# Two token norms and a layer norm whose sums over features are added up on VectorE before TensorE sums over partitions

## The reference

```python
def rms_norm(x, g):
    y = xf * lax.rsqrt(jnp.mean(xf * xf, axis=-1, keepdims=True) + EPS)
    return y * g

def first_block(x, mem, ...):
    mem_n = rms_norm(mem, mem_norm_g)
    h = rms_norm(x, norm_g[i])
    proj = h @ dn_w_in                 # then gated delta rule, cross attention to mem_n, output projection
    ...
    x = x + y @ w_out

def second_block(x, w_in, ...):
    proj = h @ w_in                    # then pooling mixer and sparse attention
    ...
    mix = concatenate([out_pool, out_attn]) @ w_out
    h = layer_norm(ALPHA * h + mix, ln1_g, ln1_b)
    ffn = peer_ffn(h, ...)             # product keys, experts; the longest stage of the kernel
    return layer_norm(ALPHA * h + ffn, ln2_g, ln2_b)

def layer_norm(x, g, b):
    mu = mean(x); var = mean(square(x - mu))
    return (x - mu) * lax.rsqrt(var + LN_EPS) * g + b
```

## Time and profile before

| | us |
|---|---|
| median of 3 runs | 3026.83 |
| lowest and highest | 3018.61 to 3031.2 |
| the profiled execution | 3026.03 |
| its span | 3024.1 |
| TensorE busy, matmul | 2846.4 (94%) |
| VectorE busy | 1903.4 (63%) |
| ScalarE busy | 1408.8 (47%) |
| GpSimd busy | 362.9 (12%) |

### The profile page before, as it was taken

How to read it: one execution, slowest core, us unless ns; L and a number is a source line. 1 busy time by engine, 2 the same in 40 slices (tenths; PEclk the granted TensorE clock), 3 DMA queues, 4 the chain that set the end, 5 groups by cost and what they waited for, 6 DMA issues and landing times.

```text
span 3024.1 us, 46453 instructions
## 1 busy us (share of the span) xinstructions
PE 2846.4 (94%) x19394; PEld 2681.0 (89%) x19394; DVE 1903.4 (63%) x2801; ACT 1408.8 (47%) x2399; POOL 362.9 (12%) x338
## 2 busy tenths in 40 slices
PE   6999998798999999999989999998999999999996
PEld 6999998687888999999988999998887899988775
DVE  5546647642333544656456855776888888878886
ACT  5346544355555433443335204433555555545554
POOL 0000010011112000002200002222122111112210
PEclk9999999899999999999999999999999999999998
DMA  4444435422232554444434458998999988889984
GB/s 185 169 157 145 171 103 178 150 98 73 78 100 94 204 181 169 167 168 158 157 127 156 152 203 312 371 362 325 366 361 363 357 326 317 324 333 345 357 338 142
DMA packets 112048, 668.47 MB, mean 221 GB/s; under 512 B 28336, under 2 KB 28552, under 8 KB 33920
## 3 DMA queue, kind: packets, MB, share of 16 engines
q1 hardware_dynamic: 86976, 496.93, 45.4%
q0 software_dynamic: 23712, 164.11, 14.8%
q10 hardware_dynamic: 1152, 4.47, 0.4%
HBM read 651.54 MB, written 13.30 MB: 220 GB/s over the span
## 4 chain that ended last, share of the span: by engine, by line
PE 66%; DVE 13%; DMA 10%; ACT 7%; issue 2%; SPq 0%; POOL 0%; DVEq 0%; ACTq 0%
PE PS L1001 66%; DMA raw<-in_pv 8%; DVE WL L1626 5%; DVE m L1617 3%; ACT WH L2304 3%; ACT m L2289 2%; DMA m<-in_pv,keep 1%; DVE m L2129 1%; ACT L2289 1%; DVE m L1817 1%; DMA raw<-in_w_kv 1%; DVE m L1814 0%; ACT m L2290 0%; PE PS L1004 0%; DVE m_896r L2222 0%
## 5 line engine op out<-in xcount | busy, mean ns | idle before, releaser
L1626 DVE TENSOR_TENSOR WL<-raw,WH 128x1024 fp32r<-128x1024 f32 x804 | 985.5, 1233 | 672.8 <-ACT WH L2304 671.9
L2304 ACT CAST WH<-raw 128x1024 fp32r<-128x1024 f32 x804 | 837.3, 1046 | 571.2 <-PE PS L1001 371.6
L1001 PE MATMUL PS<-m_4096r,WH 128*128 128x256 f32 x5184 | 997.9, 293 | 31.1 <-DVE m_4096r L1617 11.5
L1001 PEld LDWEIGHTS PS<-m_4096r,WH 128*128 128x128 f32 x5184 | 827.1, 196 | 54.7 <-issue 13.2
L1001 PE MATMUL PS<-m_4096r,WL 128*128 128x256 f32 x2592 | 743.5, 287 | 0.0
L1001 PE MATMUL PS<-m_8192r,WH 128*128 128x256 f32 (+1 forms) x2560 | 561.1, 313 | 16.7 <-issue 11.1
L1001 PE MATMUL PS<-WH,m_896r 128*128 128x512 f32 x1536 | 524.1, 394 | 24.6 <-DVE m_896r L2222 24.5
L1001 PEld LDWEIGHTS PS<-m_4096r,WL 128*128 128x128 f32 x2592 | 507.1, 196 | 0.0
L1001 PEld LDWEIGHTS PS<-m_8192r,WH 128*128 128x128 f32 x2560 | 398.6, 194 | 19.6 <-issue 11.7
L1001 PE MATMUL PS<-m_8192r,WL 128*128 128x192 f32 (+1 forms) x1792 | 405.1, 273 | 0.0
L1001 PE MATMUL PS<-WL,m_896r 128*128 128x512 f32 x1024 | 401.5, 392 | 0.0
(11 more groups left out here) (228 smaller groups left out, 1869.7 us busy)
## 6 DMA issues: line engine op xcount, KB each, us to landing
raw<-in_pu SPq DMA_DIRECT2D x128, 1024.0 KB, 6.9
raw<-in_pv SPq DMA_DIRECT2D x128, 1024.0 KB, 8.7
raw<-in_w_qkv SPq DMA_DIRECT2D x48, 1024.0 KB, 4.8
raw<-in_w_o SPq DMA_DIRECT2D x48, 1024.0 KB, 4.8
raw<-in_w SPq DMA_DIRECT2D x40, 1024.0 KB, 4.8
raw<-in_w_z SPq DMA_DIRECT2D x32, 1024.0 KB, 4.9
raw<-in_w_kv SPq DMA_DIRECT2D x16, 1024.0 KB, 4.8
raw<-in_w_q SPq DMA_DIRECT2D x16, 1024.0 KB, 4.8
```

Source lines behind the costliest of these rows:

```text
L1001: return e.matmul(o, l, x, start=start, stop=stop)
L1626: tt(WL[:, k, :], raw[:, n % NRAW, h * 1024:h * 1024 + 1024], WH[:, k, :].bitcast(F), ALU.subtract).then_inc(S["lo"], 1)
L2304: e.copy(WH[:, k, :], raw[:, n % NRAW, h * 1024:h * 1024 + 1024]).then_inc(S["hi"], 1)
```

## The change

Four tiles are added to one on VectorE with a `tensor_reduce` over a strided view (`over_tiles`: element t of tiles k, k+1, k+2, k+3, which lie 1 KB apart), and TensorE makes one matmul with ones on the result.

- First norms: `n_square` on VectorE, behind each square of ScalarE, writes a quarter's sum into `N_PART`, and `n_sum` makes 4 matmuls instead of 16. TensorE waits on `n_part`.
- Mean of six tiles: one addition over all six behind `r1` of the sixth, one matmul instead of 6.
- Statistics: for tiles 0 to 3, 4 to 7 and 8 to 11 VectorE makes two additions (deviations, squares) at the place of `stat(3)`, `stat(7)` and `stat(11)`, with two matmuls each on TensorE there; tiles 12 to 15 are summed one by one as before. 14 matmuls instead of 32. ScalarE's square into a buffer of squares waits until the additions of the four before are done.

The two lists of steps that get a new name are left out below.

```diff
--- before.py
+++ after.py
@@ -193,10 +193,9 @@
                 yield
         if first:
             self.do("begin")
-        for kt in range(16):
-            self.do("n_sum", first, kt)
-            if kt % 4 == 3:
-                yield
+        for c in range(4):
+            self.do("n_sum", first, c)
+            yield
         self.do("n_root", first)
         yield
         for c in range(4):
@@ -391,11 +390,10 @@
             yield
 
     def statistics(self, st):
-        for m in range(6):
-            while st["r"] <= m:
-                yield
+        while st["r"] <= 5:
             yield
-            self.do("mean", m)
+        yield
+        self.do("mean")
         yield
         for m in range(17):
             while m < 16 and st["r"] <= m:
@@ -611,7 +609,7 @@
     "x_high": (("n_hi", 32), ("y_hi", 9), ("x1_hi", 16), ("att_hi", 8), ("pm_hi", 8), ("h2_hi", 8)),
     "x_low": (("n_lo", 32), ("y_lo", 9), ("x1_lo", 16), ("att_lo", 8), ("pm_lo", 8), ("h2_lo", 8)),
     "small_pe": (("sg_turn", 1), ("sg_sum", 1), ("rn_sum", 1), ("bias_mm", 1), ("wi_turn", 1), ("pm", 8), ("mean", 1),
-                 ("stat", 16)),
+                 ("stat", 1)),
     "small_dve": (("sg_min", 1), ("sg_g", 1), ("sg_gc", 2), ("keep", 1), ("bias_v", 1), ("ki", 1), ("ki_copy", 1), ("wi", 1),
                   ("mask", 2), ("ln1_var", 1), ("ln1_rs", 1)),
     "small_act": (("sg_act", 7), ("rn_root", 1), ("ln1_mu", 1), ("ln1_sd", 1)),
@@ -741,6 +739,7 @@
         N_GAIN = {True: "mem_g", False: "norm_g"}
         N_BANK = {True: 2, False: 3}
         N_LOAD = {True: "mem", False: "x"}
+        N_PART = {True: f(132, 1024), False: f(136, 1024)}
         MK, MV, XQ, XA, SQ = f(112, 2048), f(120, 2048), f(64, 2048), f(132, 2048), f(80, 2048)
         MV3 = MV.rearrange("p (m c) -> p m c", m=2)
         HN_X = {"k": MK, "q": XQ}
@@ -861,6 +860,8 @@
         PING = [f(26, 256), f(28, 256)]
         PW = f(88, 2048).rearrange("p (g d) -> p g d", g=8)
         CM, MU, RS, MR = f(80, 256), f(81, 256), f(82, 256), f(83, 256)
+        SQ4 = f(84, 1024)
+        CM_PART, DEV_PART, SQ_PART = f(95, 256), f(88, 768), (f(91, 256), f(93, 256), f(94, 256))
         H2 = r(0, 8192)
         H2H, H2L = H2[:, 0:4096], H2[:, 4096:8192]
         H2_X = H2.rearrange("p (s k t) -> p s k t", s=2, t=256)
@@ -1009,10 +1010,10 @@
             def begin():
                 p.wait_ge(*at("ld_con", 32))
 
-            def n_sum(first, kt):
-                p.wait_ge(*at("n_square", kt // 4 + (1 if first else 5)))
-                t = mm(PS[:, N_BANK[first], 0:256], C("ones"), tile(TMP, kt), kt == 0, kt == 15)
-                if kt == 15:
+            def n_sum(first, c):
+                p.wait_ge(*at("n_part", c + (1 if first else 5)))
+                t = mm(PS[:, N_BANK[first], 0:256], C("ones"), tile(N_PART[first], c), c == 0, c == 3)
+                if c == 3:
                     t.then_inc(S["n_sum"], 1)
 
             def feed(n):
@@ -1487,18 +1488,27 @@
                     m = mm(PS[:, b, 0:256], PW[:, 2 * g + c, d * 128:d * 128 + 128], tile(PT_, 2 * g + c), c == 0, c == 1)
                 m.then_inc(S["pm"], 1)
 
-            def mean(m):
-                p.wait_ge(*at("r1", m + 1))
+            def mean():
+                p.wait_ge(*at("mean_part", 1))
                 p.wait_ge(*at("pm_lo", 8))
-                t = mm(PS[:, 2, 0:256], C("ones"), tile(X1, m), m == 0, m == 5)
-                if m == 5:
-                    t.then_inc(S["mean"], 1)
+                mm(PS[:, 2, 0:256], C("ones"), CM_PART, True, True).then_inc(S["mean"], 1)
 
             def stat_(m):
-                p.wait_ge(*at("dev", m + 1))
-                mm(PS[:, 2, 0:256], C("ones"), tile(X1, m), m == 0, m == 15)
-                p.wait_ge(*at("dev_sq", m + 1))
-                mm(PS[:, 3, 0:256], C("ones"), f(84 + m % 4, 256), m == 0, m == 15).then_inc(S["stat"], 1)
+                if m < 12:
+                    if m % 4 < 3:
+                        return
+                    dev, sq = tile(DEV_PART, m // 4), SQ_PART[m // 4]
+                    p.wait_ge(*at("mean", 1))
+                    p.wait_ge(*at("stat_part", m // 2 + 1))
+                else:
+                    dev, sq = tile(X1, m), tile(SQ4, m % 4)
+                    p.wait_ge(*at("dev", m + 1))
+                mm(PS[:, 2, 0:256], C("ones"), dev, m == 3, m == 15)
+                if m >= 12:
+                    p.wait_ge(*at("dev_sq", m + 1))
+                t = mm(PS[:, 3, 0:256], C("ones"), sq, m == 3, m == 15)
+                if m == 15:
+                    t.then_inc(S["stat"], 1)
 
             def h_turn(it):
                 t, c = divmod(it, 4)
@@ -1636,6 +1646,14 @@
                 lo_part(1)
                 v.wait_ge(*at("ld_con", 32))
 
+            def over_tiles(o, tiles):
+
+                return e.tensor_reduce(o, tiles.rearrange("p (k t) -> p t k", t=256), AX.X, ALU.add)
+
+            def n_square(first, c):
+                v.wait_ge(*at("n_square", c + (1 if first else 5)))
+                over_tiles(tile(N_PART[first], c), quarter(TMP, c)).then_inc(S["n_part"], 1)
+
             def n_root(first):
                 v.wait_ge(*at("n_root", 1 if first else 2))
                 v.step(recip(N_RT[first], N_RT[first]))
@@ -1967,11 +1985,21 @@
                 v.wait_ge(*at("used", done(WO2 + m)))
                 stt(tile(X1, m), tile(X1, m), ALPHA, PS[:, m % 2, 0:256], ALU.mult, ALU.add).then_inc(S["r1"], 1)
 
-            def mean(m):
-                if m == 5:
-                    v.wait_ge(*at("mean", 1))
-                    v.wait_ge(*at("att", 8))
-                    v.step(one(CM, PS[:, 2, 0:256], 1.0 / 768, ALU.mult))
+            def mean():
+                v.wait_ge(*at("r1", 6))
+                over_tiles(CM_PART, tile(X1, 0, 6)).then_inc(S["mean_part"], 1)
+                v.wait_ge(*at("mean", 1))
+                v.wait_ge(*at("att", 8))
+                v.step(one(CM, PS[:, 2, 0:256], 1.0 / 768, ALU.mult))
+
+            def stat_(m):
+
+                if m in (3, 7, 11):
+                    q = m // 4
+                    v.wait_ge(*at("dev", m + 1))
+                    over_tiles(tile(DEV_PART, q), tile(X1, 4 * q, 4)).then_inc(S["stat_part"], 1)
+                    v.wait_ge(*at("dev_sq", m + 1))
+                    over_tiles(SQ_PART[q], SQ4).then_inc(S["stat_part"], 1)
 
             def dev(m):
                 v.own()
@@ -2267,13 +2295,13 @@
...
@@ -2551,11 +2579,11 @@
                 a.wait_ge(*at("dev", m + 1))
                 a.wait_ge(*at("att", 8))
                 if m >= 4:
-                    a.wait_ge(*at("stat", m - 3))
-                act(f(84 + m % 4, 256), tile(X1, m), ACT.Square).then_inc(S["dev_sq"], 1)
+                    a.wait_ge(*at("stat_part", 2 * (m // 4)))
+                act(tile(SQ4, m % 4), tile(X1, m), ACT.Square).then_inc(S["dev_sq"], 1)
 
             def ln1():
-                a.wait_ge(*at("stat", 16))
+                a.wait_ge(*at("stat", 1))
                 act(MU, PS[:, 2, 0:256], ACT.Copy, scale=1.0 / 2048).then_inc(S["ln1_mu"], 1)
                 a.wait_ge(*at("ln1_var", 1))
                 act(RS, RS, ACT.Sqrt, bias=C("eps5")).then_inc(S["ln1_sd"], 1)
```

More of the change, by code:

```diff
@@ L2268, in end @@
                         stt(x, x, stat(16 + t), LB[:, o], ALU.mult, ALU.add).then_inc(S["out_t"], 1)
-            Plan({"prep": prep, "begin": begin, "n_root": n_root, "n_scale": n_scale, "n_split": n_split, "hn_sum": hn_sum,
+            Plan({"prep": prep, "begin": begin, "n_square": n_square, "n_root": n_root, "n_scale": n_scale, "n_split": n_split, "hn_sum": hn_sum,
                   "hn_apply": hn_apply, "mv_turn": mv_turn, "sg_pre": sg_pre, "sg_exp": sg_exp, "sg_sum": sg_sum,
@@ L2275, in vector_program @@
                   "bias": bias, "ki_out": ki_out, "index": index, "topk": topk, "v2_turn": v2_turn, "aw": aw, "an": an,
-                  "at": at_, "av": av, "pm": pm, "r1_out": r1_out, "mean": mean, "dev": dev, "ln1": ln1, "h2": h2,
+                  "at": at_, "av": av, "pm": pm, "r1_out": r1_out, "mean": mean, "dev": dev, "stat": stat_, "ln1": ln1, "h2": h2,
                   "key_top": key_top, "s_begin": s_begin, "s_cand": s_cand, "s_best": s_best, "s_place": s_place,
```

## The result

The changed kernel took 3035.73 us (median of 13 runs, 3025.41 to 3046.12), the kernel before 3026.83 us on the same chip (13 runs, 3016.46 to 3032.59): a ratio of 1.0034 with a 95% interval of 1.0019 to 1.005. It is slower by some 10 us (the medians differ by 8.9, the ratio by 10.3). That is less than the half per cent that I had named as what can be told from no change, but with 13 runs of each the interval is clear of 1. The profiled execution of it took 3041.3 us, with a span of 3039.5 us against 3024.1.

What follows compares the result with a forecast made beforehand. TensorE, busy 94% of the span and the chain for 66%, was taken as the bound. First norm 0, second norm -1.9, layer norm -0.2, clock +1.7 made -0.4 us: 3026 us, range 3018 to 3034.

Steps and rivals of the forecast that it cites:

- the first norm: First norm, of mem: sums end at 17.5 us, ScalarE asks after 20.37; value 0, cover 2.9 us.
- the second norm: Second norm, of x: VectorE becomes what ends last, its subtraction done at 52.9 instead of 54.8; gain 1.9 us.
- the waits: Second block's output projection: TensorE waits at four sums, 1.4 + 3.1 + 2.5 + 2.5 = 9.5 us, against 9.7 us saved.
- the clock: Projection: TensorE's granted clock drops behind one of three waits of 2.5 to 3.1 us, +1.7 us; ends 0 and 5.1.
- The price of an addition: VectorE: four tiles 1 KB apart taken at 1.22 us, ends 1.14 and 1.49; six tiles 1.75, ends 1.71 and 2.24.
- rival (c): Projection: the clock drops after all three pairs, additions as forecast; +3.0 us, 3029 us; chance 0.12.
- (b): VectorE's additions: a step of 1 KB makes each take 2.44 us, waits 18.6 us, 3045 us; chance 0.06.
- (a): Projection: TensorE's waits are covered after all, layer norm -6.2 us; in all about -9.5 us, 3017 us; chance 0.08.
- The range: Whole kernel's time: 3018 to 3034 us, taking in (c), the prices' upper ends and the spread between executions.

Runs made afterwards that it cites:

- the measurement: Changed kernel with all of the norms' additions but the first of each in other access patterns, only durations counting; one execution, 3038.64 us.
- the second kernel of patterns: Changed kernel with further access patterns in place of the norms' additions (8-byte step, max, two strided operands, 512 elements); one execution, 3030.21 us.
- the one with the layer norm alone: Changed kernel with the two first norms undone, only the layer norm's sums changed; 3033.13 us, ratio 1.0025 to the kernel before.
- the contiguous kernel: Changed kernel with all additions made pairwise by contiguous tensor_tensor instead of strided reduce, same places and waits; 3026.37 us, ratio 1.0005 to the kernel before.
- the last experiments: Changed kernel with TensorE making the layer norm's sums later, strided reduce kept, 3024.58 us; then with contiguous additions as well, 3011.01 us.
- norms only: Changed kernel with the layer norm's part undone, only the two first norms adding on VectorE; 3025.69 us, ratio 1.0006 to the kernel before.
- later sums: Changed kernel, strided reduce kept, TensorE making the mean's sum and the three pairs later; 3024.58 us, ratio 0.9994 to the kernel before.
- contiguous and later: Changed kernel with both contiguous pairwise additions and TensorE's layer norm sums made later; 3011.01 us, ratio 0.9948 to the kernel before.
- contiguous, filled: Kernel with contiguous additions plus 19 matmuls of constants ahead of TensorE's four waits; 3023.26 us, ratio 0.9991 to the kernel before.

## Why the prediction was wrong

The places and the mechanism were right: the first norm hidden, VectorE taking the second norm's chain, four new waits in the projection, a clock that falls behind some of them. Three sizes were off: the second norm by 1.9 us, the waits by 3.6 and the clock by 5.5, together 11.0 of the 11.5 us between the -0.4 forecast and the +11.1 measured in the projection. The first two hang on the price of an addition. The clock was taken too low by itself.

**The price of an addition.** This is the step that failed: "I take 1.22, because the strided copy shows no penalty". That copy takes 2318 ns for 2048 elements, and I compared it with what other operations need for as many. It should have been compared with a contiguous copy. The trace of before has one:

```profile
L1812 DVE COPY m<-cons x2: 680/680/681, 485.8 to 486.4; 96x1024 f32<-96x1024 f32 x2
```

680 ns for 96x1024 make some 1.3 us for 2048: at a step of 128 bytes the copy had lost nearly half of its rate. In the measurement it is the same, 1.18 us for 1024 elements at a step of 1 KB against 0.68 contiguous. So that row was no evidence that a step is free, and could not be held against the page's rule on lines of 16 bytes. It is not clear evidence for the rule either: with a step the copy only came down to what the other operations take for contiguous elements (1.18 beside 1.22 us) and not to their 1.89 or 2.02, so it may have lost only the lead that a contiguous copy has over them. No run separates the two. The measured price is 1.89 us, outside my ends of 1.14 and 1.49; the six tiles' 2.79 lay outside 1.71 to 2.24. Neither end came from a row in which each read lies far from the last (one reads contiguous elements, the other repeats elements), so they bounded the wrong thing.

**Second norm.** Forecast -1.9 us, measured 0. Four additions at 0.67 us more each are 2.7 us, which eats the gain. With additions of 1.11 us (0.68 + 0.42 in two steps) it came to -2.4, where my working had -2.2 for 1.14 us. The working is right, its price was not.

**The waits.** Forecast 1.4 + 3.1 + 2.5 + 2.5 = 9.5 us, measured 2.23 + 3.97 + 3.45 + 3.45 = 13.1. The same working with the real prices (2.79 us, and twice 1.89) gives 2.44 + 4.44 + 3.84 + 3.84 = 14.6, too long by 0.2 to 0.5 us each. VectorE's rows overlap by some 0.1 us (in the second kernel of patterns 43.03 + 1.09 lies behind the next start, 44.01) and I summed whole rows; two additions take 3.60 us of the chain, not 3.79. So the order of what is queued ahead of each sum was read well.

**The clock.** This is the second step that failed: "I count one drop among the three", 1.7 us. There were three, two of them of about 3 us, 7.2 us in all. Whether the longer waits made it worse is not settled: the same waits went with 7.2 us in the changed kernel and with 5.0 in the one with the layer norm alone. But the count was wrong without them too: in the contiguous kernel, behind 2.51, 1.98 and 1.98 us, waits shorter than the forecast's, the clock fell three times and cost some 4.5 us. That was my rival (c), 3029 us. It deserved more than the 0.12 I gave it: in the trace of before I had two gaps, and a count of one in two says little.

**The rivals.** (b) had the right direction (a step of 1 KB makes the addition dear) and place, with a price too high: 2.44 us per addition, waits 18.6, 3045 us. Both prices came out somewhat over half way from my value towards it (1.89 between 1.22 and 2.44, 2.79 between 1.75 and 3.66), and the time, 3036 us, half way between 3026 and 3045. I had let it decide by one misread row, and left its chance at 0.06 although the page spoke for it. (a), waits that are covered, did not happen; that it can be made to happen by asking later is what the last experiments show.

**The range** ended at 3034 us and should have reached to 3045: both ends of an unknown price must come from rows that share with the new operation what makes it unknown, here the step.

## What to carry to other kernels

When a sum moves from TensorE to VectorE, count the access pattern and not only the elements: adding tiles pairwise in contiguous pieces took 1.11 us where one strided reduction took 1.89. A saving on an engine that is the chain is kept only if it does not have to wait for the engine that took over the work, so move the consumer later in its queue by at least the helper's delay: in this kernel's projection that alone turned +11.1 us into -6.4, and together with contiguous additions into -9.6. And a wait on TensorE is to be priced with the clock behind it. In the kernels whose waits were 2 us and more, that added 0.4 to 0.6 of the waits' own length (5.0 and 7.2 us to 13.1, 4.5 to 7.8).

## What the runs showed of the hardware

- **Reading with a step on VectorE.** For 1024 elements of four bytes, a TENSOR_REDUCE took 1.22 us at steps of 4 and 8 bytes and 1.89 to 1.96 us at 64, 128, 256 bytes and 1 KB. Between 8 and 64 bytes nothing was measured. Per further element it is (2792 - 1894) / 512 = 1.75 ns at 1 KB. An addition of two operands went from 1.22 to 2.02 us, a copy from 0.68 (on 96 partitions) to 1.18, no more than contiguous work of the other operations.
- **Groups of two** at a step of 1 KB took 0.72 us for 512 elements, close to contiguous work (2286 ns for 2048 in the earlier trace rows is 0.57 for 512), groups of four 1.09. Not explained.
- **The clock falls behind shorter waits than I had thought, and not always.** In this projection it fell behind waits of 1.98 (twice), 2.51, 3.45 (three times of four) and 3.97 us (twice), and stayed at 1.00 behind 1.31 and 2.23 (twice). The length of the wait alone does not decide. In the second norm it was the same: behind a first wait of 2.50 us the granted clock from 42 to 46 us was 0.59 (changed kernel), 0.58 (norms only) and 1.00 (later sums), behind 1.70 to 1.72 us it was 0.70 (contiguous), 0.64 (contiguous and later) and 1.00 (contiguous, filled). The Trainium skill, page "TensorE: Matmul & The Clock Gate", section "Why this matters for your kernels", advises against gaps beyond some 3 us; two drops behind 1.98 us are against taking that as safe below.
- **Matmuls of constants as filler** kept the clock at 1.00 in the projection and made it 4.5 us shorter, though TensorE had 19 more matmuls to do.
